# Deep-norm trunk on one core: the second half's column sums on VectorE, and their matmuls behind the next stage's fourth unit

## What is computed

```python
def layer_norm(x, g, b):
    mu = jnp.mean(xf, axis=-1, keepdims=True)
    xc = xf - mu
    var = jnp.mean(xc * xc, axis=-1, keepdims=True)
    y = xc * lax.rsqrt(var + LN_EPS) * g + b

for i in range(DEPTH):
    ...
    x = layer_norm(ALPHA * x + h, ln1_g[i], ln1_b[i])
    x = layer_norm(ALPHA * x + swiglu(x, ...), ln2_g[i], ln2_b[i])
    gate = jax.nn.sigmoid(x @ ple_w_gate[i])
    x = x + gate * rms_norm(p[i] @ ple_w_proj[i], ple_norm_g[i])
```

## Time and profile before

| | us |
|---|---|
| median of 3 runs | 2708.64 (2707.30 to 2709.38) |
| the profiled execution | 2708.42 |
| its span, first to last instruction | 2706.6 |
| TensorE busy | 2625.6 |
| VectorE busy | 1475.0 |
| ScalarE busy | 945.0 |

### The profile page before, as it was taken

The page is one execution under the profiler, slowest core; times in us unless marked ns, Lnnn a source line. Parts: engine busy times, 40 slices in busy tenths (PEclk is TensorE's granted clock), DMA queues, the critical chain, the costliest instruction groups (busy, mean ns, idle before and its releaser), DMA issues. The chain is left out here.

```text
span 2706.6 us, 32719 instructions
## 1 busy us (share of the span) xinstructions
PE 2625.6 (97%) x14173; PEld 2237.0 (83%) x14173; DVE 1475.0 (54%) x1723; ACT 945.0 (35%) x1274; POOL 0.8 (0%) x7
## 2 busy tenths in 40 slices
PE   8969999999999999999999999999999969999998
PEld 7638988899787898888998888888998549888898
DVE  6998333366553564332674473332678987333265
ACT  5225322235333253222252243322355135222234
POOL 0000000000000000000000000000000000000000
PEclk9989999999999999999999999999999989999999
DMA  4101333322332223333223323333222002333322
GB/s 154 55 0 63 109 100 95 102 94 86 117 101 78 70 72 108 99 96 101 86 94 98 97 64 115 95 98 105 86 92 95 32 24 78 96 99 94 108 79 70
DMA packets 189635, 237.44 MB, mean 88 GB/s; under 512 B 14332, under 2 KB 134964, under 8 KB 189364
## 3 DMA queue, kind: packets, MB, share of 16 engines
q1 hardware_dynamic: 189492, 235.36, 27.5%
HBM read 233.21 MB, written 2.10 MB: 87 GB/s over the span
## 5 line engine op out<-in xcount | busy, mean ns | idle before, releaser
L1158 DVE TENSOR_TENSOR w_lo<-raw,w_hi 128x1024 fp32r<-128x1024 f32 x432 | 518.9, 1222 | 633.3 <-ACT w_hi L879 632.5
L879 ACT CAST w_hi<-raw 128x1024 fp32r<-128x1024 f32 x432 | 446.4, 1050 | 744.3 <-DMA raw<-in_ffn_w_up_dram 332.1
L604 PE MATMUL psum<-a_hi,w_lo 128*128 128x512 f32 x864 | 336.1, 389 | 0.0
L605 PE MATMUL psum<-a_lo,w_hi 128*128 128x512 f32 x864 | 336.1, 389 | 0.0
L606 PE MATMUL psum<-a_hi,w_hi 128*128 128x512 f32 x864 | 336.1, 389 | 0.0
L696 PE MATMUL psum<-a_hi,w_lo 128*128 128x256 f32 x1216 | 313.3, 285 | 0.0
L696 PE MATMUL psum<-a_hi,w_hi 128*128 128x256 f32 x1216 | 310.5, 283 | 0.0
L696 PE MATMUL psum<-h_hi,w_hi 128*128 128x256 f32 x1264 | 270.9, 283 | 0.0
L604 PE MATMUL psum<-h_hi,w_lo 128*128 128x512 f32 x632 | 246.2, 390 | 0.0
L606 PE MATMUL psum<-h_hi,w_hi 128*128 128x512 f32 x632 | 245.9, 389 | 0.0
L605 PE MATMUL psum<-h_lo,w_hi 128*128 128x512 f32 x632 | 245.9, 389 | 0.0
(11 more groups left out here) (230 smaller groups left out, 3864.9 us busy)
## 6 DMA issues: line engine op xcount, KB each, us to landing
raw<-in_ffn_w_gate_dram SPq DMA_DIRECT2D x176, 256.0 KB, 2.8
raw<-in_ffn_w_up_dram SPq DMA_DIRECT2D x176, 256.0 KB, 3.1
raw<-in_ffn_w_down_dram SPq DMA_DIRECT2D x176, 256.0 KB, 2.7
raw<-in_a_w_pw_dram SPq DMA_DIRECT2D x96, 256.0 KB, 2.9
raw<-in_ple_w_gate_dram SPq DMA_DIRECT2D x64, 256.0 KB, 2.8
raw<-in_b_w_in_dram SPq DMA_DIRECT2D x64, 256.0 KB, 2.9
raw<-in_c_w_in_dram SPq DMA_DIRECT2D x48, 256.0 KB, 2.9
raw<-in_b_w_out_dram SPq DMA_DIRECT2D x32, 256.0 KB, 2.8
```

The costliest lines, as they stand in the source:

```text
L604: pe.matmul(bank(grp.g, j), st_lo, mv_hi, start=(k == 0), stop=False)
L605: pe.matmul(bank(grp.g, j), st_hi, mv_lo, start=False, stop=False)
L879: act.copy(hi_u[u % RING], raw_u[u % RING]).then_inc(hi_ready, 1)
L1158: dve.tensor_tensor(lo_u[u % RING], raw_u[u % RING], hi_u[u % RING].bitcast(F32), ALU.subtract)\
```

## The change

In `stats_half` both halves now have one matmul for the column sum and one for the squares. In `half_sums_of` VectorE adds the last four tiles in half 1 too. `first_groups` calls the second half's statistics after all four units of half 0 instead of inside the third. The semaphore `half_sums` now counts two for each half.

```diff
@@ stats_half @@
-                sum_z, sum_sq = hcol(half_bank(s, h, 0), 0), hcol(half_bank(s, h, 1), 0)
-                if h == 0:
-                    pe.wait_ge(half_sums, 3 * s.norm + 1)
-                else:
-                    pe.wait_ge(first_summed, 2 * s.norm + 2)
-                    pe.wait_ge(z_pair, 4 * s.norm + 2 * h + 1)
-                last = pe.matmul(sum_z, ones[:, :], hcol(tiles(tmp, 5), h), start=True, stop=(h == 0))
-                for j in range(TILES if h == 1 else 0):
-                    pe.wait_ge(z_pair, 4 * s.norm + 2 * h + j // 2 + 1)
-                    last = pe.matmul(sum_z, ones[:, :], hcol(tiles(xf, TILES + j), h), start=False, stop=(j == TILES - 1))
-                last.then_inc(half_stats, 1)
-                pe.wait_ge(half_sums, 3 * s.norm + h + 2)
-                pe.matmul(sum_sq, ones[:, :], hcol(tiles(tmp, 4), h), start=True, stop=True).then_inc(half_stats, 1)
+                e = 2 * s.norm + h
+                pe.wait_ge(half_sums, 2 * e + 1)
+                pe.matmul(hcol(half_bank(s, h, 0), 0), ones[:, :], hcol(tiles(tmp, 5), h), start=True, stop=True)\
+                    .then_inc(half_stats, 1)
+                pe.wait_ge(half_sums, 2 * e + 2)
+                pe.matmul(hcol(half_bank(s, h, 1), 0), ones[:, :], hcol(tiles(tmp, 4), h), start=True, stop=True)\
+                    .then_inc(half_stats, 1)
@@ first_groups @@
-                    half_by_k(s, grp, ku, 0, normed, (lambda: stats_half(normed, 1)) if ku == 2 else None)
+                    half_by_k(s, grp, ku, 0, normed)
+                stats_half(normed, 1)
@@ half_sums_of @@
-                for j in range(TILES if h == 0 else 0):
+                for j in range(TILES):
```

## The result

The changed kernel takes 2718.3 us (median of 6 runs, 2717.3 to 2722.4), the kernel before 2709.0 us (median of 6 runs). The ratio is 1.0038, with a 95% interval of 1.0025 to 1.0051: slower by 9.3 us. The forecast was 2717.1 us, 8.5 us slower.

The account below looks back on a forecast made before the run. TensorE, busy 97% of the span, was taken to bound the kernel. The longer chain's +3.4 us and the clock falls' +5.1 us made +8.5 us on 2708.6 us: 2717.1 us, own range 2714 to 2721, wider range 2711 to 2725 us.

Parts of the forecast that it names:

- TensorE bounds the kernel and nothing waits for the sixth unit: Kernel before: TensorE busy 97% of the span; the sixth weight unit's low part ready 1.58 us early.
- the forecast's 13 us: Whole kernel: TensorE's busy time should fall by 13 us, less what the lower clock adds.
- The chain of 6.53 us: Second half's statistics: from the column sum's matmul until TensorE has the sixth unit's low part, 6.53 us.
- The wait for the sixth unit, 2.5 us: After the fifth unit in each of eight places, TensorE newly waits 2.5 us for the sixth unit's low part.
- The forecast of sixteen waits and 22 us: TensorE's waits view: new `w_lo` line in about sixteen places, longest 2.5 us, some 22 us in all.
- +3.4 us by the chain: Statistics' old place to first group's other half: 13.73 us after the change, +3.4 us over eight places.
- +5.1 us by the clock: Behind the new waits in eight places: four clock falls at 1.28 us each, bounds 0 and 27 us.
- four cases: Earlier TensorE idling, 1.70 plus 0.82 us (twice), 2.7 and 3.0 us: two falls, so one in two taken.
- That the clock holds: Eight places: the sixth unit's wait comes, but no clock fall or one; 2712 to 2713 us, chance 0.10.
- The faster rival: Eight places: sixth unit's low part ready in time, other half waits 0.66 us for its pair; 2695 us, chance 0.05.
- The additions set no pace: Second half's statistics: a rival had slower VectorE additions holding TensorE up, at most 3 us in all; no chance given.
- The clock's dearer falls: Eight places: longer falls, 2725 us, or falls in nearly all places, 2722 us; chance 0.12.

Follow-up runs that it names:

- the control: The kernel before, with only the sixth unit's low part and its cast moved to right behind the fifth's: 2707.6 us, ratio 0.9998.
- half the move: The whole change, but with the second half's statistics inside the fourth unit, 1.44 us earlier than in the changed kernel: 2711.7 us, ratio 1.0008.

## Why the prediction was right

*TensorE bounds the kernel and nothing waits for the sixth unit* held: `w_lo` is a new releaser after, and the control shows that 1.6 us of earliness was slack. TensorE's busy time fell by the forecast's 13 us where the clock held in the eight places (2612.5 us with the sixth unit first, against 2625.6), and by 4.0 us in the changed kernel.

*The chain of 6.53 us* held to 0.01 us: 6.52 us at 648.31. It was read from the first half, where the same instructions stand with nothing ahead of them.

*The wait for the sixth unit, 2.5 us.* The gap in the row is 2.15 or 2.16 us in the four places where TensorE also waits 0.23 us for the fifth unit, 2.26 us in one without that wait, and 2.62 us in the three places where the falls behind the first half had made TensorE late. The fifth unit's wait, forecast as 0.3 us, came in four places and not in all. The forecast of sixteen waits and 22 us is 12 and 19.7 us in the view.

*+3.4 us by the chain.* Measured by the places without a fall it is 0.53 to 0.55 us a place and not 0.44; the kernel with the wait filled has +4.2 us over the eight places (331.3 against 327.1) and +4.0 us by the medians. The term was too small by 0.6 to 0.8 us, about 0.1 us a place. The trace shows where: the matmul behind the wait has 0.22 us to the next one, where the distance is otherwise 0.12 us.

```profile
1389.38 0.39 PE L690 MATMUL psum<-a_hi,w_lo 128*128 128x256 f32 x1 [2.16 <-DVE w_lo L1153]
1389.60 0.28 PE L690 MATMUL psum<-a_hi,w_hi 128*128 128x256 f32 x1
```

So the other half starts at 1392.36, 9.50 us after the statistics, or 13.82 us after their old place and not 13.73 us; the other three places without a fall have 13.82 us too. The prediction had this restart at nothing.

*+5.1 us by the clock.* The number of falls was four, as taken. Their price was 1.39 to 1.49 us and not 1.28, so 5.8 us. By the medians the term is 5.3 us. That there were falls to pay for follows from the new wait; that one in two was right is luck. The share was a guess from four cases, and one of the four was misread. After the 2.7 us of idling at the start of the kernel the clock did not stay at 1.00: the profile has no record of it before 12.47 us, and the view puts 1.00 where it has none. The rows of before show the lower level there:

```profile
9.63 0.63 PE L595 MATMUL psum<-h_hi,w_hi 128*128 128x512 f32 x1
10.06 0.63 PE L594 MATMUL psum<-h_hi,w_lo 128*128 128x512 f32 x1
```

These are 0.43 us apart; from 14.60 on the same matmuls are 0.23 us apart. The 128x128 matmuls ahead of the idling (from 4.40) are 0.21 us apart, those from 13.49 on 0.11 us, so the clock was low before the wait as well, and the case says nothing for either side. Over the seven experiments the share went from none of eight to seven of eight. The spread of the changed kernel's runs (5 us) would hold three or four falls more or less.

*The rivals.* That the clock holds is what the filled kernel makes true by force, 2712.9 us against the 2712 to 2713 given. The faster rival, in which the weights are ready in time, is what moving the sixth unit makes true, with the wait for the first low pair that the rival named. Its time was given as 2695 us and came out at 2701.8. The rival's working left the low part's own time off VectorE's chain to the first pair: the subtraction waits for it and starts 0.82 us later, and the pair is there 9.04 us after the column sum's matmul (652.42 - 643.38) where the working had 8.24 us (652.3 - 644.06). Eight times 0.8 us is 6.4 us of the 6.8 us. The additions set no pace in the change (the mean, not VectorE, ends the wait at 649.63). The clock's dearer falls did not come: none of the four lasted longer than 3.4 us, and four places had none.

## What to carry to other kernels

Work taken off the busiest engine is worth what the chain behind it allows. Before moving a step later on a saturated engine, list what other engines do only after its result, and look there for things that have nothing to do with it, here a weight's low part in the middle of a norm. Such a passenger costs nothing while the chain starts early and becomes the bound when it starts late; moving it took two calls on VectorE and two on ScalarE. Where a wait on TensorE can't be avoided, its price is the wait and what the clock does behind it, and the two can be measured apart by filling the wait with spare matmuls.

## What was not expected of the hardware

How much the falls depend on the length of a wait. Behind a single wait of 2.62 us the clock fell in three of three places of the changed kernel and in seven of eight with only the place moved. With only the additions it fell in six of six places with a wait of 2.57 to 2.98 us and 0.30 or 0.82 us close behind it. Behind 2.15 to 2.26 us, with 0.23 us three microseconds earlier in four of the five places, it fell in one of five. Behind 0.82 and 1.19 us, in the kernel with half the move, it fell in none of eight. The length of the longest wait is not all: behind the first half's 1.70 and 0.82 us, with 0.7 us of matmuls between them, it fell in four of six places of before and the changed kernel, more often than behind the 2.15 to 2.26 us. Here the Trainium skill ("TensorE: Matmul & The Clock Gate", "Why this matters for your kernels") is right in its advice to keep TensorE's bursts together, but these runs show falls behind shorter idling than the gaps of some 3 us that it warns of.
